# Rotary positions from the projection's bank, with each tile's half swap behind the next tile

## What is computed

```python
def apply_rope_2(x, cos, sin):
    c = cos[None, :, None, :].astype(x.dtype)
    s = sin[None, :, None, :].astype(x.dtype)
    x1, x2 = jnp.split(x, 2, axis=-1)
    return jnp.concatenate([x1 * c - x2 * s, x2 * c + x1 * s], axis=-1)
```

## Time and profile before

| | us |
|---|---|
| median of 3 runs | 3044.91 (3044.56 to 3044.98) |
| the profiled execution | 3045.68 |
| its span | 3043.9 |
| mean granted TensorE clock | 0.952 of full speed |
| PE busy | 2769.8 (91%) |
| POOL busy | 1871.4 (61%) |
| ACT busy | 1490.2 (49%) |
| DVE busy | 1044.2 (34%) |

### The profile page before, as it was taken

How to read it: one execution, slowest core, us unless ns; L and a number is a source line. 1 busy time by engine, 2 the same in 40 slices (tenths; PEclk the granted TensorE clock), 3 DMA queues, 4 the chain that set the end, 5 groups by cost and what they waited for, 6 DMA issues and landing times.

```text
span 3043.9 us, 54209 instructions
## 1 busy us (share of the span) xinstructions
PE 2769.8 (91%) x19868; PEld 2566.2 (84%) x19868; DVE 1044.2 (34%) x2456; ACT 1490.2 (49%) x2604; POOL 1871.4 (61%) x789
## 2 busy tenths in 40 slices
PE   4999999999988989998889987899888899889897
PEld 2887778999976789997889987899878899778897
DVE  3124534111144521224333364333342333442334
ACT  4326744434444544444455565455545455454555
POOL 5426646878854668872458855388634588524685
PEclk8999999999998999998999998999999999989998
DMA  6224434545533445541235533255423355313453
GB/s 237 90 70 146 139 111 139 180 162 183 184 112 111 166 137 182 186 153 63 98 126 183 181 118 109 92 170 182 138 77 111 106 184 179 125 56 111 135 182 125
DMA packets 115044, 421.48 MB, mean 138 GB/s; under 512 B 12768, under 2 KB 13792, under 8 KB 114400
## 3 DMA queue, kind: packets, MB, share of 16 engines
q1 hardware_dynamic: 114336, 413.39, 40.5%
q10 hardware_dynamic: 576, 6.23, 0.5%
HBM read 418.52 MB, written 1.05 MB: 138 GB/s over the span
## 4 chain that ended last, share of the span: by engine, by line
issue 43%; PE 28%; POOL 25%; DVE 3%; ACT 1%; POOLq 1%; ACTq 0%; DVEq 0%
POOL ring_low L1922 25%; PE bank L544 8%; PE bank L545 8%; PE bank L546 8%; PE bank L725 1%; PE bank L752 1%; PE bank L660 1%; PE bank L657 1%; POOLq L1925 0%; DVE rstd L1416 0%; PE bank L768 0%; ACT ring_high L1014 0%; PE bank L739 0%; ACT scr L1111 0%; POOLq L1921 0%
## 5 line engine op out<-in xcount | busy, mean ns | idle before, releaser
L1922 POOL TENSOR_TENSOR ring_low<-ring,ring_high 128x1024 fp32r<-128x1024 f32 x785 | 1871.2, 2405 | 1150.0 <-ACT ring_high L1014 790.0
L544 PE MATMUL bank<-high,ring_high 128*128 128x256 f32 (+1 forms) x4052 | 1210.1, 299 | 148.6 <-DVE low L1478 73.0
L545 PE MATMUL bank<-low,ring_high 128*128 128x256 f32 (+1 forms) x4052 | 1191.5, 294 | 0.0
L546 PE MATMUL bank<-high,ring_low 128*128 128x256 f32 (+1 forms) x4052 | 1190.5, 294 | 0.0
L544 PEld LDWEIGHTS bank<-high,ring_high 128*128 128x128 f32 x4052 | 800.5, 198 | 172.8 <-DVE low L1478 77.3
L545 PEld LDWEIGHTS bank<-low,ring_high 128*128 128x128 f32 x4052 | 800.6, 198 | 10.8 <-issue 1.2
L546 PEld LDWEIGHTS bank<-high,ring_low 128*128 128x128 f32 x4052 | 799.8, 197 | 8.7
L1212 ACT ACTIVATE ring_high<-ring 128x1024 fp32r<-128x1024 f32 x462 | 479.0, 1051 | 33.9 <-PE bank L544 33.9
L1014 ACT ACTIVATE ring_high<-ring 128x1024 fp32r<-128x1024 f32 x323 | 334.7, 1052 | 124.6 <-PE bank L544 93.5
L544 PE MATMUL bank<-hid_high,ring_high 128*128 128x256 f32 x1232 | 351.0, 285 | 9.7 <-DVE hid_low L1683 9.7
L545 PE MATMUL bank<-hid_low,ring_high 128*128 128x256 f32 x1232 | 350.3, 284 | 0.0
(11 more groups left out here) (177 smaller groups left out, 2970.1 us busy)
## 6 DMA issues: line engine op xcount, KB each, us to landing
ring<-in_units SPq DMA_DIRECT2D x785, 512.0 KB, 3.3
...
```

Source lines behind the costliest of these rows:

```text
L544: first = pe.matmul(out, w[0], x[0], start=start, stop=False, **more)
L545: pe.matmul(out, w[0], x[1], start=False, stop=False, **more)
L546: return first, pe.matmul(out, w[1], x[0], start=False, stop=stop, **more)
L1922: pool.tensor_tensor(whole(ring_low, u), whole(ring, u), whole(ring_high, u).bitcast(fp32), ALU.subtract).then_inc(unit_ready, 1)
```

## The change

The copies of tiles that are rotated go from ACT to DVE, which forms both products from the projection's bank in two instructions (`spin`): minus-signed sine product into a scratch slot (`turned`), cosine product into the tile. PE swaps the sine product instead of the tile (a swap of the halves and multiplication by a sine of the other sign commute), and DVE adds the bank to the tile (`rope`, one instruction). In blocks 0 and 1 ACT still copies the context's half of the tiles (`context_half`), and DVE waits for that before it reads the same bank. PE issues the swap of a tile behind a later tile's matmuls: in block 0 three tiles later, elsewhere one. In block 1 and layers 0 and 3 the values are projected after the queries; the weight stream is packed in that order. In these three the key swaps stand behind query tile 0, and query tile 7's swap behind the values. `values` releases owed weight slots at some of its matmuls; in layers 0 and 3 ACT feeds twice more in the attention, after item 1 (`late`). The calls of `evacuate` take a range and a number for the scale; those for memory and cross attention are otherwise unchanged and left out here.

```diff
+        def turned(slot):
+            return scr[:, 4096 + T * (slot % 4):4096 + T * (slot % 4) + T]
...
-                def rotate(st, m, src):
+                def rotate(st, m, slot=0):
                     b = 4 + m % 2
                     claim(b)
                     pe.wait_ge(*when(st, "out", m))
-                    pe.matmul(banks[b][:, 0:T], const("swap", P), src, start=True, stop=True
+                    pe.matmul(banks[b][:, 0:T], const("swap", P), turned(slot + m), start=True, stop=True
                               ).then_inc(*mark(rot_ready, st, "rot", m))
-                    reader[b] = (st, "rotread", m)
+                    reader[b] = (st, "rope", m)
...
+                                if at < len(blocks) - 1:
+                                    release(mm)
...
+                def turn_ab(m):
+                    if m - 3 in ROT0:
+                        rotate("ab", m - 3)
+                project("ab", UNITS["ab"], 16, split(0, 2 * T), 2 * T, ready=lambda k: ("n01", "h", k), after=turn_ab)
                 project_v("ab", UNITS["ab"] + 16, 4, tokens(0, 2 * T), 4)
-                for m in ROT0:
-                    rotate("ab", m, (Q2 if m < 8 else K2)(m % 8)[:, 0:T])
...
+                def turn_behind(q, k):
+                    def after(m):
+                        if m == 0:
+                            rotate(k, 0, 2)
+                            rotate(k, 1, 2)
+                        else:
+                            rotate(q, m - 1)
+                    return after
                 project("c_k", UNITS["c_in"], 2, split(0, 2 * T), 2 * T, ready=lambda k: ("n11", "h", k))
-                for m in range(2):
-                    rotate("c_k", m, K2(m)[:, 0:T])
-                project_v("c_v", UNITS["c_in"] + 2, 1, tokens(0, 2 * T), 4)
-                project("c_q", UNITS["c_in"] + 4, 8, split(0), T)
-                for m in range(8):
-                    rotate("c_q", m, Q1(m))
+                project("c_q", UNITS["c_in"] + 2, 8, split(0), T, after=turn_behind("c_q", "c_k"))
+                project_v("c_v", UNITS["c_in"] + 10, 1, tokens(0, 2 * T), 4)
+                rotate("c_q", 7)
                 c_needs = ([("c_q", "rope", m) for m in range(8)]
-                           + [("c_k", "rope", 1), ("c_k", "out", 1), ("c_v", "vout", 3)])
...
-                        for m in range(2):
-                            rotate(st + "k", m, K1(m))
-                        project_v(st + "v", u + 2, 1, tokens(0), 2)
-                        project(st + "q", u + 4, 8, split(0), T)
-                        for m in range(8):
-                            rotate(st + "q", m, Q1(m))
+                        project(st + "q", u + 2, 8, split(0), T, after=turn_behind(st + "q", st + "k"))
+                        project_v(st + "v", u + 10, 1, tokens(0), 2)
+                        rotate(st + "q", 7)
...
-                        rotate(st + "d", 5, K1(8))
                         stats(st + "cq", None, tiles=3)
+                        rotate(st + "d", 5)
                         stats(st + "ckv", None, tiles=2)
                         project(st + "uq", UNITS[st + "_uq"], 12, split(0), T, depth=3, per_unit=2,
-                                ready=lambda k: (st + "cq", "h", k))
-                        for m in range(4):
-                            rotate(st + "uq", 8 + m, Q1(8 + m))
+                                ready=lambda k: (st + "cq", "h", k),
+                                after=lambda m: rotate(st + "uq", m - 1) if m > 8 else None)
                         up = lambda k: split(0)(4 + k)
                         project(st + "uk", UNITS[st + "_ukv"], 8, up, T, depth=2, per_unit=4,
-                                ready=lambda k: (st + "ckv", "h", k))
+                                ready=lambda k: (st + "ckv", "h", k),
+                                after=lambda m: rotate(st + "uq", 11) if m == 0 else None)
...
+                def context_half(st, tiles, dst, u0, scale=1.0):
+                    for m in tiles:
+                        feed(u0 + m)
+                        act.wait_ge(*when(st, "proj", m))
+                        act.activation(dst(m)[:, T:2 * T], banks[m % 4][:, T:2 * T], ACT.Copy, scale=scale
+                                       ).then_inc(*mark(act_done, st, "half", m))
+                def feed_each(u0, n):
+                    for m in range(n):
+                        feed(u0 + m)
...
+                        if s == 1 and late is not None:
+                            feed(late)
...
-                evacuate("ab", 16, lambda m: (Q2 if m < 8 else K2)(m % 8), UNITS["ab"],
-                         scale=lambda m: -HD ** -0.5 if m < 8 else 1.0)
+                context_half("ab", range(0, 4), Q2, UNITS["ab"], scale=-HD ** -0.5)
+                evacuate("ab", range(4, 8), Q2, UNITS["ab"], scale=-HD ** -0.5)
+                context_half("ab", range(8, 12), lambda m: K2(m - 8), UNITS["ab"])
+                evacuate("ab", range(12, 16), lambda m: K2(m - 8), UNITS["ab"])
...
-                evacuate("c_k", 2, K2, UNITS["c_in"])
-                evacuate("c_q", 8, Q1, UNITS["c_in"] + 4, scale=lambda m: -HD ** -0.5)
+                context_half("c_k", range(2), K2, UNITS["c_in"])
+                feed_each(UNITS["c_in"] + 2, 8)
...
-                        evacuate(st + "k", 2, K1, UNITS[st])
-                        evacuate(st + "q", 8, Q1, UNITS[st] + 4, scale=lambda m: -HD ** -0.5)
-                        attention(st + "t", gqa_items(256, swa_masks, True, COLS["sinks_a"] + 16 * (l // 3)))
+                        feed_each(UNITS[st], 10)
+                        attention(st + "t", gqa_items(256, swa_masks, True, COLS["sinks_a"] + 16 * (l // 3)),
+                                  late=UNITS[st] + 11)
...
-                        evacuate(st + "d", 6, lambda m: K1(8) if m == 5 else spare(m), UNITS[st + "_down"])
+                        evacuate(st + "d", range(5), spare, UNITS[st + "_down"])
+                        feed(UNITS[st + "_down"] + 5)
...
-                        evacuate(st + "uq", 12, Q1, UNITS[st + "_uq"], per_unit=2, scale=lambda m: -192 ** -0.5)
-                        evacuate(st + "uk", 8, K1, UNITS[st + "_ukv"], per_unit=4)
+                        evacuate(st + "uq", range(8), Q1, UNITS[st + "_uq"], per_unit=2, scale=-192 ** -0.5)
+                        feed_each(UNITS[st + "_uq"] + 4, 2)
+                        evacuate(st + "uk", range(8), K1, UNITS[st + "_ukv"], per_unit=4)
...
-                def rope(st, m, x, kind):
-                    b = 4 + m % 2
+                def spin(st, m, x, kind, scale=1.0, slot=0, halved=False):
+                    dve.wait_ge(*when(st, "proj", m))
+                    if halved:
+                        dve.wait_ge(*when(st, "half", m))
+                    b = banks[m % 4][:, 0:T]
+                    dve.scalar_tensor_tensor(out=turned(slot + m), in0=b, scalar=-scale, in1=const("sin" + kind, T),
+                                             op0=ALU.mult, op1=ALU.mult)
+                    dve.scalar_tensor_tensor(out=x, in0=b, scalar=scale, in1=const("cos" + kind, T),
+                                             op0=ALU.mult, op1=ALU.mult).then_inc(*mark(dve_done, st, "out", m))
+                def rope(st, m, x):
                     dve.wait_ge(*when(st, "rot", m))
-                    s = scr[:, 4096 + T * (m % 4):4096 + T * (m % 4) + T]
-                    dve.tensor_tensor(s, banks[b][:, 0:T], const("sin" + kind, T), ALU.mult
-                                      ).then_inc(*mark(dve_done, st, "rotread", m))
-                    link(dve.tensor_tensor(x, x, const("cos" + kind, T), ALU.mult))
-                    dve.tensor_tensor(x, x, s, ALU.add).then_inc(*mark(dve_done, st, "rope", m))
+                    dve.tensor_tensor(x, banks[4 + m % 2][:, 0:T], x, ALU.add).then_inc(*mark(dve_done, st, "rope", m))
+                def spin_queries(q, k, keys, kind):
+                    for m in range(8):
+                        spin(q, m, Q1(m), kind, scale=-HD ** -0.5)
+                        if m == 0:
+                            rope(k, 0, keys(0))
+                            rope(k, 1, keys(1))
+                        else:
+                            rope(q, m - 1, Q1(m - 1))
...
+                for group, scale in ((ROT0[0:4], -HD ** -0.5), (ROT0[4:8], 1.0)):
+                    for m in group:
+                        spin("ab", m, (Q2 if m < 8 else K2)(m % 8)[:, 0:T], "_ax", scale=scale, halved=True)
+                    for m in group:
+                        rope("ab", m, (Q2 if m < 8 else K2)(m % 8)[:, 0:T])
                 evacuate_v("ab", 16, lambda n: V(n % 4, 256 * (n // 4), 256 * (n // 4) + 256))
-                for m in ROT0:
-                    rope("ab", m, (Q2 if m < 8 else K2)(m % 8)[:, 0:T], "_ax")
...
-                    rope("c_k", m, K2(m)[:, 0:T], "_ax")
+                    spin("c_k", m, K2(m)[:, 0:T], "_ax", slot=2, halved=True)
```

(24 more changed lines are left out.)

18 lines of the change are left out of this document (9 added, 9 removed).

## The result

| | before | after |
|---|---|---|
| median, us | 3044.73 (3044.05 to 3044.98, 4 runs) | 3019.76 (3015.25 to 3021.25, 4 runs) |
| the profiled execution, us | 3045.68 | 3018.34 |
| its span, us | 3043.9 | 3016.2 |
| mean granted clock | 0.952 | 0.957 |

The ratio is 0.9916 [0.9899, 0.9933]: faster by 25 us, 0.8%. Forecast were 3002 and a range of 2990 to 3018, so the time lies 1.8 us above the range. The mechanism of the rotation came out as forecast; most of what the clock was to give did not.

What follows compares the result with a forecast made beforehand. TensorE is busy 91% of 3043.9 us, so time is won only where it stands still or runs slowly; 5.6 + 20.2 + 9 + 4.5 + 7.6 - 4 = 42.9 us off the median gave 3002, range 2990 to 3018.

Steps and rivals of the forecast that it cites:

- Term 1: Block 0: the 10.18 us rope gap before the scores goes, inline swaps and the last value copy replace it; gain 5.6 us.
- Term 2: Block 1, layers 0 and 3: rope gaps before the scores go, 5.6 us each, key swaps 1.1 each; together 20.2.
- Term 3: Layer 2: the norm and POOL's weight units start 2.2 us earlier and the 3.70 us wait goes; gain 9 us.
- The swap's price: A swap moved inside a projection costs TensorE 0.43 us, with bounds 0.30 and 0.60.
- C: Inline swaps cost 0.9 us instead of 0.43, 33 swaps by 0.47 making 15.5, so 3018 us; chance 0.1.
- D: POOL holds VectorE's new rotation instructions, 7.4 us per tile against TensorE's 3.3, time near 3099 us; chance 0.03.
- Term 4: Block 0's attention start runs at full instead of half clock; of some 6.4 us saved, 4.5 kept.
- Term 5: Attentions of layers 0 and 3 run at full clock, 5.8 us each, less 2 for the late feed; gain 7.6.
- Rival A: The clock falls in the attentions despite the short gap, from waits for first exponentials; about 3014 us; chance 0.2.
- Term 6: Block 1's attention loses a prefetched unit, TensorE stands 5.9 us and the clock falls behind it; costs 4 us, bounds nothing to 7.8.

## Why the prediction was wrong

By its terms, against the profiled executions:

- **Term 1**, block 0's ropes: 5.6 forecast, 5.96 measured. **Term 2**, block 1 and layers 0 and 3: 6.7 each, measured 6.09, 6.27 and 6.56. **Term 3**, layer 2: 9, measured 9.6, and by its own steps: the run of POOL's units comes 2.7 us earlier against the down projection (2.2 forecast), and from there to the scores 30.35 us became 23.43, 6.9 won (6.8 forecast). **The swap's price** of 0.43: 0.42. Rivals C (0.9 per swap) and D (VectorE held) are refuted by the two views of the changed kernel above. C was also priced too low: it counts 33 swaps inline where the change puts 40, and 40 by 0.47 would have been 3021, outside the range.
- **Term 4**, block 0's clock: 4.5, measured 3.13 in one execution and 4.23 in the other. The clock falls for 3.4 us or not, at waits of 0.80 and 1.14 us for ring_low.
- **Term 5 is the step that failed.** Its price was right: it put layer 0's attention at full clock and without the late feed at 37.24 - 5.8 = 31.4 us, and six runs took 31.3. The late feed cost 3.0 instead of 2. But the clock was to stay up because the gap is short, read from two attentions that stay at 1.00, after 0.98 us in layer 2 and, by the trace, 0.47 in the memory attention. That was an inference from the gap alone. Layers 0 and 3 have three waits in their first item (1.19, 0.47 and 1.16 us, of which the last is 0.59 to 0.71 in layer 0 once the clock has fallen), and with the values last the clock fell among or behind them in ten attentions of twelve. Filled with matmuls that nothing reads, it never fell there, in eight such attentions, nor in two with the values in the middle; these kept it without the matmuls too, so the waits are part of the cause and not all of it. Measured gain: 0.0 and -0.1 instead of 7.6. Rival A had this, at 0.2, though it also gave up block 0's clock, of which 3.1 came.
- **Term 6 was mis-sized.** The lost prefetch was seen, with the unit, the engine and the wait (5.9 us forecast, 4.72 measured, since the clock was down already), and priced at 4. It cost 9.3 in one execution and 4.2, as forecast, in the other. In both the fall came before the wait, not behind it; what differs is how long the half clock lasted behind the wait's end: 12.4 us in the one, 4.5 in the other. "Nothing, up to 7.8" was too narrow for the first; why the two differ is open. With one unit more, the loss is gone.
- What the sum lacked, 15.6 us (42.9 forecast, 27.3 between the profiled executions), is so made up: term 5 7.7, term 6 5.3, term 4 1.4, term 2 1.3 (its three times 6.7 are 20.1, not 20.2), elsewhere 0.9, less 1.0 that terms 1 and 3 gave above the forecast. The rest of the 17.8 between 3002 and 3019.76 is how the two profiled executions stand to their medians.
- The range held A with block 1 at its forecast price (3014), but not with term 6 as it came out: 3014 and 5.3 are 3019. That this is near the 3019.8 measured is in part luck: the 3.1 of block 0's clock, which A gave up and which came, nearly cancels the 2.2 by which the profiled executions stand apart from their medians and the 0.9 lost elsewhere.
- In the whole the forecast of 3002 is, by its number, the time of another kernel, the one with the values left in the middle (3000.0 and 3002.0). The prediction counted what moving the values last hides, and not against it what it takes from the feed: it gains 3.5 us and costs, feed and clock together, 9.4 in block 1 and 5.9 and 5.3 in layers 0 and 3.
